# Token-wise norms, a shared convolution chunk and reordered casts in a two-block transformer kernel

## What is computed

```python
def rms_norm(x, g):
    y = x * lax.rsqrt(jnp.mean(x * x, axis=-1, keepdims=True) + EPS)
    return y * g

for l in range(DEPTH):                       # 2 layers
    x = x + 0.5 * swiglu(rms_norm(x, ffn1_norm[l]), ...)
    h = rms_norm(x, mix_norm[l])
    a, g, q, k, v = jnp.split(h @ w_in[l], splits, axis=-1)   # 5 x 512 columns

    u = a * jax.nn.sigmoid(g)                # convolution branch, 512 channels
    y = depthwise_causal_conv(u, conv_w, 31 taps) + conv_b
    conv_out = jax.nn.silu(rms_norm(y, conv_norm))            # over the channels

    q = rms_norm(q, q_norm[l])               # over each head's 64 columns
    k = rms_norm(k, k_norm[l])               # 4 heads x 2 maps of 64
    s = q @ k.T * scale + bias               # causal, per head and map
    p = softmax(s)
    o = (p[map 0] - lam * p[map 1]) @ v
    o = rms_norm(o, subln_g) * (1 - lam_init)

    x = x + jnp.concatenate([conv_out, o], -1) @ w_out[l]
    x = x + 0.5 * swiglu(rms_norm(x, ffn2_norm[l]), ...)
```

## Time and profile before

| what | us |
|---|---|
| median of 3 runs (lowest, highest) | 1809.97 (1809.88, 1811.41) |
| the profiled execution's own time | 1811.22 |
| its span in the trace | 1809.4 |
| PE busy | 1758.0 (97%) |
| DVE busy | 1208.4 (67%) |
| ACT busy | 911.7 (50%) |
| POOL busy | 287.7 (16%) |
| chain that ended last | PE 87%, DVE 8%, ACT 3%, issue 1% |

### The profile page before, as it was taken

One profiled execution on the slowest core, in us unless ns is written; L12 is line 12 of the kernel. 1 busy time (PEld: TensorE's weight loads), 2 busy tenths in 40 slices (PEclk: granted clock), 3 DMA queues, 4 the chain that ended last, 5 costly groups with the idle time before them and its releaser, 6 DMA issues.

```text
span 1809.4 us, 25402 instructions
## 1 busy us (share of the span) xinstructions
PE 1758.0 (97%) x9839; PEld 1502.4 (83%) x9839; DVE 1208.4 (67%) x1594; ACT 911.7 (50%) x1221; POOL 287.7 (16%) x155
## 2 busy tenths in 40 slices
PE   8999999999999999999999998999999999989999
PEld 7757888899897788878888977888888889778887
DVE  5756766778676775576665794666666667946665
ACT  4544444545455444445445656544554456565443
POOL 2000300376241040000000741000000006410000
PEclk9999999999999999999999999999999999999999
DMA  9223655554502576535554432655465554316552
GB/s 302 102 70 124 220 191 186 152 181 156 198 1 83 156 238 194 188 129 195 194 193 163 164 116 70 209 185 188 161 209 185 186 185 164 117 47 209 192 194 102
DMA packets 203965, 293.95 MB, mean 162 GB/s; under 512 B 6426, under 2 KB 169728, under 8 KB 203888
## 3 DMA queue, kind: packets, MB, share of 16 engines
q1 hardware_dynamic: 200768, 285.62, 47.6%
q0 software_dynamic: 2688, 6.47, 1.4%
q10 hardware_dynamic: 432, 0.79, 0.1%
HBM read 291.81 MB, written 1.05 MB: 162 GB/s over the span
## 4 chain that ended last, share of the span: by engine, by line
PE 87%; DVE 8%; ACT 3%; issue 1%; DMA 0%; POOL 0%; SPq 0%; ACTq 0%; DVEq 0%
PE acc L1864 27%; PE pg L1864 15%; PE pg L1927 12%; PE pg L1931 12%; PE pg L1930 6%; PE pg L1928 6%; PE acc L2338 1%; DVE acc L1743 1%; PE pg L2134 1%; ACT w_hi L793 1%; DVE w_lo L1252 1%; PE pg L2322 1%; PE pg L2324 1%; DVE stats L1307 1%; PE pg L1975 1%
## 5 line engine op out<-in xcount | busy, mean ns | idle before, releaser
L1252 DVE TENSOR_TENSOR w_lo<-w_raw,w_hi 128x2048 fp32r<-128x2048 f32 x231 | 539.1, 2334 | 182.2 <-ACT w_hi L793 170.6
L793 ACT CAST w_hi<-w_raw 128x2048 fp32r<-128x2048 f32 x270 | 515.6, 1910 | 68.5 <-PE pg L1864 25.2
L1864 PE MATMUL acc<-w_hi,op 128*128 128x512 f32 x1536 | 496.6, 394 | 8.2 <-DVE op L1829 6.4
L1927 PE MATMUL pg<-op,w_hi 128*128 128x512 f32 x960 | 383.2, 399 | 7.7 <-DVE op L1278 3.8
L1931 PE MATMUL pg<-op,w_hi 128*128 128x512 f32 x960 | 380.8, 397 | 0.0
L1864 PEld LDWEIGHTS acc<-w_hi,op 128*128 128x128 f32 x1536 | 290.4, 189 | 70.0 <-issue 12.6
L1864 PE MATMUL acc<-w_lo,op 128*128 128x512 f32 x768 | 300.7, 392 | 0.0
L695 POOL TENSOR_TENSOR w_lo<-w_raw,w_hi 128x2048 fp32r<-128x2048 f32 x39 | 179.8, 4613 | 743.5 <-DVE w_lo L1252 615.4
L1930 PE MATMUL pg<-op,w_lo 128*128 128x256 f32 x960 | 267.9, 279 | 0.0
L1928 PE MATMUL pg<-op,w_lo 128*128 128x256 f32 x960 | 267.0, 278 | 0.0
L1864 PE MATMUL pg<-op,w_hi 128*128 128x256 f32 x1232 | 229.2, 286 | 2.8 <-DVE op L1278 1.2
(11 more groups left out here) (314 smaller groups left out, 1845.2 us busy)
## 6 DMA issues: line engine op xcount, KB each, us to landing
w_raw<-in_mlp_w SPq DMA_DIRECT2D x64, 1024.0 KB, 5.5
w_raw<-in_ffn_w_gate SPq DMA_DIRECT2D x44, 1024.0 KB, 5.1
w_raw<-in_ffn_w_up SPq DMA_DIRECT2D x44, 1024.0 KB, 5.1
w_raw<-in_ffn_w_down SPq DMA_DIRECT2D x44, 1024.0 KB, 4.8
w_raw<-in_ssm_w_in SPq DMA_DIRECT2D x24, 1024.0 KB, 5.3
w_raw<-in_w_in SPq DMA_DIRECT2D x20, 1024.0 KB, 5.0
w_raw<-in_attn_w_in SPq DMA_DIRECT2D x9, 1024.0 KB, 9.2
w_raw<-in_ssm_w_out SPq DMA_DIRECT2D x8, 1024.0 KB, 4.8
```

Of the source, the lines that this page charges most:

```text
L793: act.copy(w_hi[:, u % RING, :], w_raw[:, u % RING, :]).then_inc(hi_ready, 1)
L1252: dve.tensor_tensor(w_lo[:, s, :], w_raw[:, s, :], w_hi[:, s, :].bitcast(F32), ALU.subtract) \
L1864: ins = pe.matmul(psum, l, r, start=first and i == 0, stop=last and i == 2)
L1927: pe.matmul(bank, hi, joined, start=k == 0, stop=False)
```

## The change

Six edits. After the change line numbers differ, as given in brackets.

1. The mix norm: DVE writes X times rstd (token tile 0 as one instruction of 1024 columns, tile 1 as four of 256), and PE transposes.
2. Query and key norms by token: PE sums squares with the squares as the stationary side and a two-column matrix as the moving one (`qk_sums`, four matmuls, line 2148); root and reciprocal work on 128 x 8. The query's norm becomes a scalar on the scores, whose take is split into two instructions, one for each query tile. For keys ACT spreads the 128 x 8 values to 128 x 512 (`head_expand`), PE turns them (`key_spread`, four matmuls, line 2161), and DVE multiplies the keys (`key_norm`).
3. The last convolution chunk: PE does 20 of its 31 taps (four in a step, line 2501), DVE the other 11, so that TAPS adds up to 104 and not 93. `convolve_last` joins both in step 4, not 5.
4. The convolution norm by token: ACT squares the four chunks at once in step 5; PE sums by token (8 matmuls with one moving column, line 2510) at the end of step 6; root and reciprocal work on 128 x 2; PE spreads the result (two matmuls, line 2516) and DVE multiplies.
5. ACT copies the turned mixture before the exponentials of the step, not after them.
6. First attention: ACT's two weight casts stand in steps 14 and 16, behind the copy and `pair_hi`; DVE's in steps 15 and 17.

The diff, cut to its core:

```diff
--- before.py
+++ after.py
...
-TAPS = [24, 22, 8, 8, 8, 8, 5, 5, 5]
-PE_TAPS = 6
-DIAGS = [0, 10, 20, CK]
-assert sum(TAPS) == 3 * CK
+TAPS = [24, 23, 10, 11, 8, 10, 6, 6, 6]
+PE_TAPS = 4
+PE_CONV = 20
+DIAGS = [0, 8, 16, PE_CONV]
+assert sum(TAPS) == 4 * CK - PE_CONV
...
+            def head_expand(l, n):
+
+                i = 4 * l + n - 4
+                act.wait_ge(qk_rstd, i + 1)
+                act.copy(hexp[:, i // 2 % 2, :].rearrange("p (k n) -> p k n", n=HD),
+                         hdev[:, i % 2, :].unsqueeze(2).broadcast_to([P, 8, HD])).then_inc(qk_exp, 1)
...
-                if s == AQ + 2:
-                    split(U_ATT_OUT + 2)
-                if s == AQ + 7:
-                    split(U_ATT_OUT + 3)
                 if AQ <= s - 3 < AQ + BH:
                     turned_head(s - 3)
                 if s >= 13 and s % 2 == 1:
                     pair_hi((s - 5) // 2)
+                if s == 14:
+                    split(U_ATT_OUT + 2)
+                if s == 16:
+                    split(U_ATT_OUT + 3)
...
-                        act.activation(acc[:, i % 2, :], acc[:, i % 2, :], ACT.Sqrt, bias=lnb[:, 1:2],
-                                       scale=1.0 / HD).then_inc(qk_std, 1)
+                        if i >= 2:
+                            act.wait_ge(qk_rstd, i - 1)
+                        if n % 2:
+                            act.activation(hdev[:, i % 2, :], acc[:, 0, 0:8], ACT.Sqrt, bias=lnb[:, 1:2],
+                                           scale=1.0 / HD).then_inc(qk_std, 1)
+                        else:
+                            act.activation(hdev[:, i % 2, :], acc[:, 0, 0:8], ACT.Sqrt, bias=lnb[:, 2:3],
+                                           scale=1.0 / HD / SCALE ** 2).then_inc(qk_std, 1)
                     elif n >= 8:
+                        if n == 8:
+                            head_expand(l, 7)
...
+                    if s >= 6 and s % 2 == 0:
+                        h = DH * l + (s - 6) // 2
+                        act.wait_ge(mixT_done, h + 1)
+                        if h >= 2:
+                            act.wait_ge(o2_done, h - 1)
+                        act.copy(pmixT[:, h % 2, :], pg[:, 2, 0:384]).then_inc(mixT_ready, 1)
                     if s < 2 * DH:
                         act.wait_ge(mx2_ready, i + 1)
                         b = s % 4
...
-                    if s == 6:
+                    if s == 5:
 
                         act.wait_ge(pe_conv, l + 1)
-                        act.wait_ge(cconv, 4 * l + 3)
-                        act.activation(osq[:, 0:3, :], cacc[:, 0:3, :], ACT.Square).then_inc(csq, 1)
-                    if s == 7:
                         act.wait_ge(cconv, 4 * l + 4)
-                        act.activation(osq[:, 3, :], cacc[:, 3, :], ACT.Square).then_inc(csq, 1)
+                        act.activation(osq, cacc, ACT.Square).then_inc(csq, 1)
                     if s == 8:
                         act.wait_ge(csum, l + 1)
-                        act.activation(acc[:, 0, 0:T], acc[:, 0, 0:T], ACT.Sqrt, bias=lnb[:, 1:2],
+                        act.activation(cdev, acc[:, 0, 0:TT], ACT.Sqrt, bias=lnb[:, 1:2],
                                        scale=1.0 / CCH).then_inc(cstd, 1)
...
-                dve.tensor_scalar(diag[:, t, :], ident[:, :], rstd[:, t:t + 1], None, ALU.mult) \
-                    .then_inc(norm_ready, 1)
+                parts = KC // 2 if t else 1
+                w = D // parts
+                for i in range(parts):
+                    dve.tensor_scalar(xn[:, t, i * w:(i + 1) * w], X[:, t, i * w:(i + 1) * w], rstd[:, t:t + 1], None,
+                                      ALU.mult).then_inc(norm_ready, 1)
...
-                if s == AQ + 3:
-                    split(U_ATT_OUT + 2)
-                if s == AQ + 8:
-                    split(U_ATT_OUT + 3)
                 if s >= 13 and s % 2 == 1:
                     pair_lo((s - 5) // 2)
+                if s == 15:
+                    split(U_ATT_OUT + 2)
+                if s == 17:
+                    split(U_ATT_OUT + 3)
...
-                    bc = COL["conv_b"] + 4 * l + 3
-                    dve.tensor_scalar(cacc[:, 3, :], pg[:, 3, 0:T], pcol[:, bc:bc + 1], None, ALU.add).then_inc(cconv, 1)
+                    link.all_but(0)
+                    dve.tensor_tensor(cacc[:, 3, :], pg[:, 3, 0:T], cacc[:, 3, :], ALU.add).then_inc(cconv, 1)
...
+                def head_rstd(n):
                     i = 4 * l + n - 4
                     dve.wait_ge(qk_std, i + 1)
-                    link(dve.reciprocal(acc[:, i % 2, :], acc[:, i % 2, :]))
+                    dst = hdev[:, i % 2, :] if n % 2 else qr[:, i // 2 % 2, :]
+                    dve.reciprocal(dst, hdev[:, i % 2, :]).then_inc(qk_rstd, 1)
+
+                def key_norm(n):
+                    j = 2 * l + (n - 5) // 2
+                    dve.wait_ge(qk_spread, j + 1)
                     dst = head_pair(n)
-                    dve.tensor_tensor(dst, dst, acc[:, i % 2, :], ALU.mult).then_inc(qk_ready, 1)
+                    dve.tensor_tensor(dst, dst, acc[:, 1, :], ALU.mult).then_inc(qk_ready, 1)
...
+                convolve_on(1)
+                head_rstd(4)
+                convolve_on(2)
+                head_rstd(5)
+                convolve_on(3)
+                head_rstd(6)
+                key_norm(5)
+                convolve_on(4)
+                head_rstd(7)
                 convolve_on(5)
+                key_norm(7)
+                dve.wait_ge(qk_rstd, 4 * l + 4)
...
-                        dve.scalar_tensor_tensor(out=prob2[:, b, :], in0=pg[:, s % 2, 0:384], scalar=SCALE,
-                                                 in1=rbias[:, h, :], op0=ALU.mult, op1=ALU.add) \
-                            .then_inc(sc2_taken, 1)
+                        for a, z, qt in ((0, P, 0), (P, 384, 1)):
+                            r = ((h % 2) * TT + qt) * 2 + s % 2
+                            ins = dve.scalar_tensor_tensor(out=prob2[:, b, a:z], in0=pg[:, s % 2, a:z],
+                                                           scalar=qr[:, h // 2, r:r + 1], in1=rbias[:, h, a:z],
+                                                           op0=ALU.mult, op1=ALU.add)
+                        ins.then_inc(sc2_taken, 1)
...
-                link(dve.reciprocal(acc[:, 0, 0:T], acc[:, 0, 0:T]))
+                dve.reciprocal(cdev, cdev).then_inc(crstd, 1)
+                dve.wait_ge(cspread, l + 1)
                 for a in range(2):
                     dve.tensor_tensor(osq[:, 2 * a:2 * a + 2, :], cacc[:, 2 * a:2 * a + 2, :],
-                                      acc[:, 0, 0:T].unsqueeze(1).broadcast_to([P, 2, T]), ALU.mult).then_inc(cnorm, 1)
+                                      acc[:, 1, 0:T].unsqueeze(1).broadcast_to([P, 2, T]), ALU.mult).then_inc(cnorm, 1)
...
-                pe.matmul(acc[:, i % 2, :], blk_const("halves"), sq[:, i % 2, :], start=True, stop=True) \
-                    .then_inc(qk_sum, 1)
+                if i:
+
+                    pe.wait_ge(qk_std, i)
+                for c in range(2):
+                    for t in range(TT):
+                        o = c * T + t * P
+                        k = (c * TT + t) * 2
+                        ins = pe.matmul(acc[:, 0, k:k + 2], sq[:, i % 2, o:o + P], blk_const("halves")[:, ::HD],
+                                        start=True, stop=True)
+                ins.then_inc(qk_sum, 1)
+
+            def key_spread(j):
+
+                pe.wait_ge(qk_exp, j + 1)
+                if j:
+
+                    pe.wait_ge(qk_ready, j)
+                for c in range(2):
+                    for t in range(TT):
+                        k = (c * TT + t) * 2
+                        ins = pe.matmul(acc[:, 1, c * T + t * P:c * T + t * P + P],
+                                        hexp[:, j % 2, k * HD:(k + 2) * HD], ident[:, :], start=True, stop=True)
+                ins.then_inc(qk_spread, 1)
...
+                    if n in (7, 9):
+                        key_spread(2 * l + (n - 7) // 2)
...
-                        for k in range(PE_TAPS * s, min(PE_TAPS * (s + 1), CK)):
+                        for k in range(PE_TAPS * s, min(PE_TAPS * (s + 1), PE_CONV)):
...
+                    if s == 6:
+
+                        pe.wait_ge(csq, l + 1)
+                        for t in range(TT):
+                            for c in range(4):
+                                ins = pe.matmul(acc[:, 0, t:t + 1], osq[:, c, t * P:(t + 1) * P], ones_m,
+                                                start=c == 0, stop=c == 3)
+                        ins.then_inc(csum, 1)
                     if s == 2 * DH:
-
-                        pe.wait_ge(csq, 2 * l + 2)
-                        for c in range(4):
-                            ins = pe.matmul(acc[:, 0, 0:T], ones_m, osq[:, c, :], start=c == 0, stop=c == 3)
-                        ins.then_inc(csum, 1)
```

(10 more changed lines are left out.)

49 lines of the change are left out of this document (23 added, 26 removed).

## The result

The changed kernel takes **1823.22 us** in the median of 6 runs (1820.61 to 1824.9), the kernel before 1810.23 beside it: 13.0 us slower, ratio 1.0068, 95% interval 1.0055 to 1.0081. Forecast were 1816.0 and 6.0 slower, with a range up to 1820.5. The direction is right and the size is not: 13.0 us against 6.0, and outside the range. A second measurement gave 1822.79 against 1810.93, so 11.9 slower (ratio 1.0057, 1.0044 to 1.0071).

The account below looks back on a forecast made before the run. PE was taken to bound the kernel (87% of the chain). Per layer 0.5 + 0.3 + 0.5 + 4.2 - 0.05 = 5.5, twice 11.0, with -5.0 +6.0: 1816.0 us against the median of 1809.97, range 1807.0 to 1820.5.

Parts of the forecast that it names:

- First attention: Moved weight casts shorten two PE waits and end the low clock behind them: -5.0 us, ends -1.9 and -5.9.
- Mix turn: DVE's tile 0 instruction grows from 0.29 to 0.81 us, delaying the last residual addition: +0.5 us per layer.
- rival D: As forecast, plus low clock behind the mix turn, 1.6 us per layer: 1819.2 us; chance 0.12.
- Projection: Narrow matmuls for query and key sums and key spreads lengthen PE's path: scores of step 0 start 2.0 us later.
- first take: DVE's first reading of scores, no longer late without four long reciprocals: moves by +0.3 us per layer.
- Rival C: Narrow matmuls cost about 0.05 us per record, by their moving columns: 1801.5 to 1806 us; chance 0.13.
- Softmax steps: More DVE taps and split takes against a shorter stalled negation: eighth take, seen alone, +0.5 us per layer.
- The sums: Convolution norm's sums before step 7's scores wait for squares, then run at low clock: +4.2 us per layer.
- Rival B: Same waits but PE's clock stays full: no change, 1810 us (1808 to 1813.5); chance 0.24.
- Tail: Last exponentials to first output matmul, old sums gone, spread and hand-overs added: -0.05 us per layer, ends -2.5 and +1.

Follow-up runs that it names:

- e1: The kernel before with edit 6 alone (order of four weight casts in the first attention): 1806.22 us against 1811.24.
- e4: The changed kernel with the mix norm as before (rstd on a diagonal, PE multiplies): 1818.05 us, ratio 1.0036 to the kernel before.
- e8: The changed kernel unaltered, measured and traced a second time: 1822.79 us against 1810.93 for the kernel before.
- e2: The changed kernel with the convolution norm's sums one step later, behind the scores of step 7 and the first head output: 1816.53 us.
- e3: The changed kernel with ten dummy matmuls (128x512, bf16) on PE in front of its wait for the squares: 1817.34 us.
- e5: The changed kernel with edit 4's sums undone (old form behind the score loop, no spread; squares stay in step 5): 1807.51 us against 1810.93.
- e9: The changed kernel with the convolution norm's token sums at the old sums' place, the spread behind the second head output: 1813.67 us.
- e10: The changed kernel with edits 1 and 4 undone, plus dummy matmuls at PE's long mix-stage waits and behind the first block's layer-norm turns: 1801.43 us.
- e11: e10 with edit 3 undone too (PE does all 31 taps of the last chunk, six a step), squares in step 6: 1802.41 us.

## Why the prediction was wrong

- **First attention, -5.0.** Right: -4.5 in the stages, -5.0 in e1. Not foreseen was a low clock behind the next turn, at 152; it stands in e1, e4, e8 and the change, costs 0.9 us in these (181.4 against 180.5 us from there to the turn at 333), and is absent in e2, e3, e5 and e9, which have edit 6 too. In all of these and in the kernel before PE waits the same 1.74 us ahead of it; what decides between them is open.
- **Mix turn, +0.5.** The wait itself came to +0.20 and +0.25, half of the term; the sentence "PE has as many records as before" was beside the point. PE's waits grew from 0.27 and 0.59 to 1.30 and 1.14 us, and the clock fell behind them: +1.3 per layer, in the row of the projection. That is rival D, to which I gave 0.12 as a case of its own. e4 shows it. D's time of 1819.2 is still too short: it adds one stretch per layer to the forecast, and not the others.
- **Projection, +2.0, and first take, +0.3.** Right: +2.0 at full clock (62.70 against 60.72), 8 narrow records 0.95 us, and the loss is taken back by DVE, which no longer comes late. Rival C, cheap narrow matmuls, is refuted. One moving column costs what 64 did, 1.84 us for 16 records in e3. The Trainium skill (TensorE: Matmul & The Clock Gate, "LDWEIGHTS") is borne out by it.
- **Softmax steps, +0.5.** Right in sum (+0.66) and in the stall (0.96 left, as against 2.94). What I missed is the clock. I wrote that PE would wait 1 us in each step and took it for harmless; it waits nowhere up to step 4, and 0.47 and 1.76 us behind its last taps, and there the clock falls. e10 and e11 show that it falls with edit 3 and not without. The Trainium skill's warning (TensorE: Matmul & The Clock Gate, "HAM oscillation"), that pauses between bursts leave each burst cold, fits this row too, and I had used it for one place only.
- **The sums, +4.2.** Right in size: +4.49. e3 splits it as forecast, 5.1 us at full clock. But the cause of the low clock was another than I wrote. I had the wait for the squares bring it down; it was down at 1075.0, 0.6 us before that wait began, and it falls at this step in e5 and e10 too, where no sums stand there. That the price fits is in part luck. Rival B, a full clock at this place, is refuted: the level is 0.50 there, where I had priced 0.57.
- **Tail, -0.05.** Right as a mean of +0.26 and -0.19. But the sum ended at the first output matmul. Behind it the weight matmuls, on PE's own path, paid +1.01 and +0.77: the kernel before is at the low level there for some 3 us (0.59 in 1092 to 1096), the change for some 5 (0.50 in 1096 to 1100, 0.71 in 1100 to 1104). I had costed that stage at nothing.
- **The step that failed** is the sum's treatment of the clock: one low stretch was priced, at one place, and D was set beside it as a rival. The stretches add up: 1.3 and 0.9 per layer and 0.9 behind the attention are 5.3 of the 6.4 us by which the span grew more than forecast; another 0.9 is the later start of this execution, which is chance. The range failed with it, because it took each for an alternative. On its other side the prediction says that the range leaves out most of C; C's times, 1801.5 to 1806, lie outside it altogether.

## What to carry to other kernels

On a kernel that is bound by PE, price each new wait of PE twice, once as the wait, and once as the matmuls behind it at half the clock, also when these are weights of the next stage; such terms add up, and each place with gaps gets its own. Before taking work off PE in a step that another engine bounds, ask what it was good for: here 31 taps as matmuls kept the clock that 20 lost, and ten dummy matmuls in a wait of 3 us brought 1.1 us in one row. A sum whose result is wanted late must not stand in front of work that is wanted now, least of all with a wait on a third engine.

## What was unexpected of the hardware

The clock went down for 1.30 and 1.14 us of waiting around a turn of 1.23 us (stretch 992 to 996, 0.64), in 10 of 12 such turns, and did not for 0.27 and 0.59 (e4, 1.00); these waits are shorter than the 1.91 us and more that I had taken for a lower bound. How long the low level lasts was unexpected too: from about 1075 to 1092 without a break, though PE was busy for all 4.00 us of 1080 to 1084 with matmuls of one moving column and scores. Under ten dummy matmuls (128x512, bf16) it ended sooner: they take 2.36 us at full clock and 3.33 in e3, where the clock is 0.52 in 1074 to 1075 and 1.00 in the next. The page's row of the clock shows the change's stretches, two slices of the span in layer 1 among them, where that of the kernel before has nines only:

```profile
PEclk9999999999999999999999989999999999889999
```
